# Joined softmax maps in attention C, output weights loaded early, and an MLP that writes its rows token by token

## The chip, the core and the metric

The kernel runs on one core of a Trainium2 chip. The metric is device time in microseconds (us) of one launch, the median of several executions. Engines are named as the profile names them: PE is TensorE, DVE VectorE, ACT ScalarE, POOL GpSimd, SP the sync engine that issues the DMAs.

## The reference, cut to what matters

Two layers over 1024 tokens of width 1024, all in float32. Each layer has four kinds of attention heads side by side (A, B, C, D), an output projection, and an MLP.

```python
for l in range(2):
    h = rms_norm(x, norm_mix_pre[l])
    ua, ub, uc, ud = jnp.split(h @ w_in[l], SPLITS, axis=-1)
    oa, ob, oc, od = attention A, B, C, D of ua, ub, uc, ud    # each normed
    mix = jnp.concatenate([oa, ob, oc, od], axis=-1) @ w_out[l]
    x = x + rms_norm(mix, norm_mix_post[l])
    h = rms_norm(x, norm_mlp_pre[l])
    f = jnp.square(jax.nn.relu(h @ w_up[l])) @ w_down[l]       # 1024 -> 4096 -> 1024
    x = x + rms_norm(f, norm_mlp_post[l])
```

Attention C is the one that the change rewrites. Each of its 4 heads has two softmax maps over the same values, with a bias that falls with distance:

```python
lam = exp(sum(lq1 * lk1)) - exp(sum(lq2 * lk2)) + lambda_init
sc  = einsum('bhmqd,bhmsd->bhmqs', q, k) * scale - slopes * dist   # m = 0, 1
p   = softmax(sc, axis=-1)
a   = p[:, :, 0] - lam * p[:, :, 1]
o   = einsum('bhqs,bhsd->bqhd', a, v)
```

## The kernel before

The program is a row of stages, each a block in which every engine has its own instruction list; the lists are tied together by counting semaphores, and every stage ends in a barrier of all engines (`end_stage`). There is no planner: the order on each engine is the order in which the Python code writes it. The layer loop runs twice. In it come the projection and attention of A, then two passes (head pairs) of the projection and attention of C, two of D, then B, then the output stage, the MLP stage and a norm stage.

float32 products are made of halves. A value is split into a high half (a rounded copy in the type fp32r) and a low half (value minus high half), and a product is three passes: high by high, high by low, low by high. ACT makes high halves, DVE or POOL the low ones. A matmul streams 512 columns past a 128 x 128 stationary tile.

**Attention C** (`attention_stage` with `combine`). A pass has 2 heads with 2 maps each, so 4 maps of 8 query tiles: 32 map tiles. For each, PE makes 128 x 1024 scores (two matmuls) in PSUM. DVE adds the bias and takes the maximum in one operation (L605). ACT takes the exponential and its row sum (L574). PE transposes the eight 128 x 128 parts (L293), in two pieces of four. ACT and DVE split each piece (L558, L616). PE multiplies by the values, for two query tiles at a time (L519), and folds (L532). At the end of a map, DVE scales by the row sums (L628) and, after the second map of a head, joins the two outputs with lambda (L630).

**The stage before attention C** (`pair_stage`). PE makes three units of 128 output columns from the layer's input and weights that come over a ring of two slots. SP issues the weights, then `extra_dma`: the distance table of 1920 columns (L976), the slopes (L977), and the lambda vectors (L979 to L981). ACT makes the two bias tables from it (`biases`, L987), and only then the first high half `c_p_h` (L925). SP waits for that half and then issues 32 copies that stack the halves for the score products (L897). The stage waits for the last of them.

**Output stage.** `mix` holds a token tile of 128 tokens and 1024 features at a time. Each tile is squared, summed by head group, scaled (`mix_sums`, `mix_norm`), transposed by PE (`turn_mix`) and split (`mix_high`, `mix_low`). w_out comes in eight blocks over a ring of three (L1445), is scaled by the gains and split by ACT and DVE (`weight_high` L1527, `weight_low` L1623). PE multiplies tiles 0 and 1 together block by block while the weights come, then tiles 2 to 7 one by one. Behind each product follow a norm, the addition to x (`post_norm`, L1630 and L1635), a second norm (`pre_norm`, L1643), a transposition and a split for the MLP. DVE begins its list with a wait for eleven small loads of gains.

**MLP stage.** In each of 4 chunks of 1024 hidden columns there are 8 up units and 8 down units, each of 48 matmuls, all with a weight tile stationary and activations streamed, so that results have features on the partitions. After an up unit follow relu (ACT, L1758), square (DVE, L1772) and the split (L1761, L1775). After a down unit DVE adds to `mlp_out_t` (L1782). Weights of 128 columns come over a ring of two slots, split by ACT (L232) and POOL (L241).

**Norm stage** (`norm_stage`, tag `mlp_post`). It loads x and the gains, PE transposes `mlp_out_t` back to tokens, and for each of 8 token tiles follow the norm (L400), the addition to x (L405), the next layer's norm (L413), a transposition, and the split (L386, L419).

## Time and profile before

| | us |
|---|---|
| median of 3 runs | 3611.39 (3608.26 to 3613.09) |
| the profiled execution | 3608.68 |
| its span, first to last instruction | 3607.0 |

| engine | busy us | share |
|---|---|---|
| PE | 3198.7 | 89% |
| DVE | 1512.7 | 42% |
| ACT | 1347.0 | 37% |
| POOL | 437.0 | 12% |

The mean granted clock of PE is 0.932 of full speed. It has two levels, 1.2 and 2.4 GHz. Shares are means over stages with different limits. The windows below say how busy each engine is in one stage; the order of instructions in time says what it waits for.

### The profile page before, as it was taken

Reading aid. Unit: us, or ns where it says so; the run is one execution under the profiler, and the core shown is the slowest. Engines: PE = TensorE matmul, PEld = TensorE weight load, DVE = VectorE, ACT = ScalarE, POOL = GpSimd, SP = SyncE. Lnnn points to the kernel's source line nnn. Section 1 sums busy time; section 2 is a strip of 40 time slices with the busy share of each in tenths; the row PEclk is TensorE's granted clock in tenths of the full one; section 3 lists DMA queues with packets and bytes.
Section 4 is the critical chain, followed back from the end, with each engine's and each line's share of the span. In section 5 each row is a group of like instructions: output and inputs, shape, how many; then the busy total and the mean of one; then the engine's idle time right before and its main releaser. Section 6 shows DMA issues by size and latency. Waiting matters only on the chain. (4 is left out here: it accounts for less than half of the span.)

```text
span 3607.0 us, 41597 instructions
## 1 busy us (share of the span) xinstructions
PE 3198.7 (89%) x16304; PEld 2668.6 (74%) x16304; DVE 1512.7 (42%) x1975; ACT 1347.0 (37%) x2210; POOL 437.0 (12%) x209
## 2 busy tenths in 40 slices
PE   7789888878789999999769889888878899999996
PEld 5678776767568888888658777776766688888885
DVE  4848554366542111112358476443765311111115
ACT  3648553455322121212227466443653221211113
POOL 1000000110002222222110000001100122222220
PEclk9899999889899999999879999898889999999998
DMA  5030333100321111111230312331012211111112
GB/s 151 1 76 1 77 64 64 28 15 7 105 70 47 47 47 46 52 47 47 105 65 1 76 30 48 64 64 34 10 32 91 65 53 47 47 47 47 46 52 105
DMA packets 250646, 191.32 MB, mean 53 GB/s; under 512 B 65480, under 2 KB 229320, under 8 KB 250442
## 3 DMA queue, kind: packets, MB, share of 16 engines
q1 hardware_dynamic: 250494, 189.38, 19.5%
q8 instruction: 95, 1.56, 0.2%
q14 instruction: 45, 0.37, 0.0%
q10 hardware_dynamic: 12, 0.02, 0.0%
HBM read 141.12 MB, written 24.89 MB: 46 GB/s over the span
## 5 line engine op out<-in xcount | busy, mean ns | idle before, releaser
L241 POOL TENSOR_TENSOR w_l_m<-w_raw_m,w_h_m 128x1024 fp32r<-128x1024 f32 (+2 forms) x136 | 313.6, 2306 | 1655.5 <-ACT w_h_m L232 1655.5
L249 PE MATMUL u_ps<-h_hi,w_h_m 128*128 128x512 f32 x1024 | 406.9, 397 | 17.3 <-POOL w_l_m L241 17.3
L250 PE MATMUL u_ps<-h_lo,w_h_m 128*128 128x512 f32 x1024 | 407.3, 398 | 0.0
L250 PE MATMUL u_ps<-up_l,w_h_m 128*128 128x512 f32 x1024 | 398.4, 389 | 0.0
L249 PE MATMUL u_ps<-up_h,w_h_m 128*128 128x512 f32 x1024 | 398.4, 389 | 0.0
L232 ACT ACTIVATE w_h_m<-w_raw_m 128x1024 fp32r<-128x1024 f32 (+2 forms) x136 | 135.9, 1004 | 578.7 <-PE u_ps L253 562.5
L1782 DVE TENSOR_TENSOR mlp_out_t<-mlp_out_t,u_ps 128x1024 f32<-128x1024 f32 x64 | 78.1, 1221 | 591.8 <-PE u_ps L253 591.8
L253 PE MATMUL u_ps<-h_hi,w_l_m 128*128 128x512 f32 x1024 | 323.1, 397 | 0.0
L253 PE MATMUL u_ps<-up_h,w_l_m 128*128 128x512 f32 x1024 | 315.3, 389 | 0.0
L1772 DVE TENSOR_TENSOR m_square<-m_relu 128x1024 f32<-128x1024 f32 x64 | 78.4, 1226 | 515.5 <-ACT m_relu L1758 515.5
L249 PEld LDWEIGHTS u_ps<-h_hi,w_h_m 128*128 128x128 f32 x1024 | 193.8, 189 | 64.3 <-POOL w_l_m L241 18.1
L1758 ACT ACTIVATE m_relu<-u_ps 128x1024 f32<-128x1024 f32 x64 | 65.6, 1025 | 467.8 <-PE u_ps L253 467.8
L250 PEld LDWEIGHTS u_ps<-h_lo,w_h_m 128*128 128x128 f32 x1024 | 193.5, 189 | 47.3
L253 PEld LDWEIGHTS u_ps<-h_hi,w_l_m 128*128 128x128 f32 x1024 | 193.5, 189 | 47.0
L249 PEld LDWEIGHTS u_ps<-up_h,w_h_m 128*128 128x128 f32 x1024 | 192.3, 188 | 40.1
L253 PEld LDWEIGHTS u_ps<-up_h,w_l_m 128*128 128x128 f32 x1024 | 192.2, 188 | 40.0
L250 PEld LDWEIGHTS u_ps<-up_l,w_h_m 128*128 128x128 f32 x1024 | 192.1, 188 | 40.0
L616 DVE TENSOR_TENSOR pt_l_c<-t_ps_c,pt_h_c 128x512 fp32r<-128x512 f32 x256 | 165.3, 685 | 17.4 <-ACT pt_h_c L558 16.6
L605 DVE CUSTOM_DVE_ANT_0 s_ps_c<-s_ps_c,alibi 128x1024 f32<-128x1024 f32 x128 | 157.0, 1229 | 15.1 <-PE s_ps_c L493 13.6
L574 ACT ACTIVATE prob_c<-s_ps_c,nmax_c 128x1024 f32<-128x1024 f32 x128 | 143.2, 1119 | 26.1 <-DVE nmax_c L605 26.1
L293 PE MATMUL t_ps_c<-ident,prob_c 128*128 128x128 f32 x1024 | 144.9, 285 | 8.8 <-DVE pt_l_c L616 8.1
L293 PEld LDWEIGHTS t_ps_c<-ident,prob_c 128*128 128x128 f32 x1024 | 120.8, 146 | 40.2 <-issue 23.3
(298 smaller groups left out, 6474.3 us busy)
## 6 DMA issues: line engine op xcount, KB each, us to landing
w_raw_m<-in_w_down SPq DMA_DIRECT2D x64, 512.0 KB, 4.0
w_raw_m<-in_w_up SPq DMA_DIRECT2D x56, 512.0 KB, 4.0
ow_raw<-in_w_out SPq DMA_DIRECT2D x16, 512.0 KB, 3.7
mix<-out_x SPq DMA_DIRECT2D x16, 512.0 KB, 4.4
out_x<-mix SPq DMA_DIRECT2D x16, 512.0 KB, 4.0
x_mlp_post<-out_x SPq DMA_DIRECT2D x16, 512.0 KB, 8.9
out_x<-x_mlp_post SPq DMA_DIRECT2D x16, 512.0 KB, 2.6
x_mix_pre<-in_x SPq DMA_DIRECT2D x8, 512.0 KB, 8.2
```

The costliest lines, as they stand in the source:

```text
L232: last = nc.scalar.activation(hi[0:rows, u % 2, cols, :], raw[0:rows, u % 2, cols, :], ACT.Copy)
L241: last = nc.gpsimd.tensor_tensor(lo[0:rows, u % 2, cols, :], raw[0:rows, u % 2, cols, :], hi[0:rows, u % 2, cols, :], ALU.subtract)
L249: nc.tensor.matmul(o, w_hi, x_hi[:, tok], start=first, stop=False)
L250: nc.tensor.matmul(o, w_hi, x_lo[:, tok], start=False, stop=False)
L253: ins = nc.tensor.matmul(o, w_lo, x_hi[:, tok], start=False, stop=last)
L293: last = nc.tensor.transpose(dst[:, i * P:(i + 1) * P], src_of(i), ident[:, :])
L574: nc.scalar.activation(prob[:, n % 2, 0:cnt * P], s_ps[:, n % 2, 0:cnt * P], ACT.Exp, scale=1.0 if tiles[n % NT][2] is None else -1.0, bia ...
L605: nc.vector.tensor_tensor_reduce(out=s, in0=s, in1=bias(m), scale=1.0, scalar=MIN_START, op0=ALU.add, op1=ALU.min, accum_out=nmax[:, n:n + ...
L616: nc.vector.tensor_tensor(pt_l[at], turned(p, k0, k1), pt_h[at], ALU.subtract) \
L1758: nc.scalar.activation(r_sb[:, :], u_ps[:, u % 2, :], ACT.Relu) \
L1772: nc.vector.tensor_tensor(s_sb[:, :], r_sb[:, :], r_sb[:, :], ALU.mult) \
L1782: nc.vector.tensor_tensor(ft[:, m, :], ft[:, m, :], u_ps[:, u % 2, :], ALU.add) \
```

## The change

1. Attention C gets a stage of its own, `difference_stage`. Both maps of a head are taken together for each query tile. Two scores, two maxima and two exponentials are made. DVE computes the ratio of lambda and the two row sums (`weigh`: a reciprocal and a `scalar_tensor_tensor` of one column). POOL multiplies the second map by it and adds the first, 1024 columns each. From there on one map is transposed, split, and multiplied by the values. There is one scaling for each head and no joining of outputs.
2. `extra_dma` of C loads the distance table twice, straight into the two bias tables, and `biases` scales them in place.
3. w_out is loaded whole during attention B (`fetch_w_out`, on SP).
4. In the output stage `mix_sums(0)` comes ahead of the wait for the small loads. Tile 0 is multiplied alone: first the two passes with high halves of the weights, then the pass with the low ones. All other tiles follow one by one. The first up unit's weights are loaded and split here.
5. The MLP has 8 chunks of 512 hidden columns. Up units are as before. The down products have activations stationary (128 tokens) and weights streamed (512 columns), so that results have tokens on the partitions; DVE collects them in `acc` by 512 columns. w_down comes in full rows. In the last chunk the norms, the addition to x, the transpositions and the splits follow each token tile. The norm stage behind the MLP is gone.

```diff
+        def difference_stage(maps, bias, mix_cols, mix, lam):
+            TURN_LAG, VALUE_LAG = 2, 4
+                    scores(0, 0)
+                    scores(0, 1)
+                    for n in range(n_all + VALUE_LAG + 1):
+                        if n + 1 < n_all:
+                            scores(n + 1, 0)
+                        if 0 <= n - TURN_LAG < n_all:
+                            turn(n - TURN_LAG, 0)
+                            turn(n - TURN_LAG, 1)
+                        if n + 1 < n_all:
+                            scores(n + 1, 1)
+                        s = n - VALUE_LAG
+                        if s >= 1 and s % 2 == 0:
+                            finish(s // 2 - 1)
+                        if 0 <= s < n_all:
+                            values(s // 2, s % 2)
...
+                @block.gpsimd
+                def _(pool):
+                    for n in range(n_all):
+                        pool.wait_ge(S["ratio_done"], n + 1)
+                        nc.gpsimd.tensor_scalar(second[:, n % 2, :], second[:, n % 2, :], ratio[:, 1, n:n + 1], 1.0,
+                                                ALU.mult, ALU.mult).then_inc(S["scaled"], 1)
+                        pool.wait_ge(S["scaled"], n + 1)
+                        nc.gpsimd.tensor_tensor(first[:, n % 3, :], first[:, n % 3, :], second[:, n % 2, :],
+                                                ALU.add).then_inc(S["combined"], 1)
...
+                    def weigh(n):
+
+                        dve.wait_ge(S["exp_done"], 2 * n + 2)
+                        after(nc.vector.reciprocal(ratio[:, 0, n:n + 1], z[:, 1, n:n + 1]))
+                        nc.vector.scalar_tensor_tensor(out=ratio[:, 1, n:n + 1], in0=z[:, 0, n:n + 1], scalar=lam,
+                                                       in1=ratio[:, 0, n:n + 1], op0=ALU.mult, op1=ALU.mult) \
+                            .then_inc(S["ratio_done"], 1)
...
+                    for n in range(n_all + VALUE_LAG + 1):
+                        if n + 1 < n_all:
+                            maximum(n + 1, 0)
+                        if n < n_all:
+                            weigh(n)
+                        if n + 1 < n_all:
+                            maximum(n + 1, 1)
+                        if 0 <= n - TURN_LAG < n_all:
+                            low(n - TURN_LAG, 0)
+                            low(n - TURN_LAG, 1)
...
-                            sp.dma_start(nd[:, :], a["distance"]).then_inc(S["const_landed"], 16)
+                            for j in range(2):
+                                sp.dma_start(alibi[:, j, :], a["distance"]).then_inc(S["const_landed"], 16)
...
+                        def fetch_w_out(sp):
+                            for k in range(KT):
+                                sp.dma_start(wo_raw[:, k, :], a["w_out"][layer][k * P:(k + 1) * P, :]) \
+                                    .then_inc(S["w_landed0"], 16)
...
                         turn_mix(0)
+                        pe.wait_ge(S["tt_lo"], 1)
+                        for k in range(KT):
+                            pe.wait_ge(S["w_hi"], k + 1)
+                            passes_of(0, k, ((h_hi, w_h), (h_lo, w_h)))
                         turn_mix(1)
-                        pe.wait_ge(S["tt_lo"], 2)
                         for k in range(KT):
-                            if k == KT // 2:
-                                turn_mix(2)
                             pe.wait_ge(S["w_lo"], k + 1)
-                            for t in range(2):
-                                last = products_of(t, k)
-                                if k == KT - 1:
-                                    last.then_inc(S["gemm_done"], 1)
-                        turn_mix(3)
-                        for t in range(2, NT):
+                            last = passes_of(0, k, ((h_hi, w_l),))
+                        last.then_inc(S["gemm_done"], 1)
+                        turn_mix(2)
+                        for t in range(1, NT):
...
+                    def down(ch, t, ks):
+                        d0 = 2 * t
+                        tok = slice(t * P, (t + 1) * P)
+                        done = 2 * NT * ch + d0
+                        if ks[0] == 0 and done >= 4:
+                            pe.wait_ge(S["acc_done"], done - 2)
+                        for k in ks:
+                            pe.wait_ge(S["up_lo"], ch * CK + k + 1)
+                            pe.wait_ge(S["d_lo"], ch * CK + k + 1)
+                            for lhs, rhs in ((up_h, d_h), (up_h, d_l), (up_l, d_h)):
+                                for n in range(2):
+                                    last = nc.tensor.matmul(d_ps[:, (d0 + n) % 4, :], lhs[:, k, tok],
+                                                            rhs[:, k, n * HALF:(n + 1) * HALF],
+                                                            start=(k == 0 and rhs is d_h and lhs is up_h),
+                                                            stop=(k == CK - 1 and lhs is up_l))
...
+                    for ch in range(CH):
+                        for u in range(CK):
+                            up(ch * CK + u)
+                        down(ch, 0, range(0, CK - 1))
+                        down(ch, 1, range(0, CK - 1))
+                        down(ch, 0, range(CK - 1, CK))
+                        down(ch, 1, range(CK - 1, CK))
+                        for t in range(2, NT):
+                            down(ch, t, range(CK))
+                            if ch == CH - 1 and t >= H_LAG:
+                                if t == H_LAG:
+                                    pe.wait_ge(S["relu_done"], NU)
+                                turn(t - H_LAG)
+                    for s in range(NT - H_LAG, NT):
+                        turn(s)
...
+                    for ch in range(CH):
+                        for k in range(ch * CK, ch * CK + CK):
+                            down_hi_weights(k)
+                        for n in range(ch * CK, ch * CK + CK):
+                            rectify(n)
...
-                norm_stage("mlp_post", ft, vec("norm_mlp_post"), vec("norm_mix_next"))
```

## Rows read from the trace of the kernel before

**Rows 1.** Windows: attention C, attention D, MLP. Busy us (instructions) by engine, clock, DMA.

```profile
core 0: us, PE busy (x) PEld busy (x) DVE busy (x) ACT busy (x) POOL busy (x), PEclk, DMA share, GB/s
268.00:363.00 95.00, 87.02 (x640) 77.59 (x640) 82.32 (x138) 75.22 (x144) 0.00 (x0) 0.95 0.00 1
...
556.00:584.00 28.00, 25.13 (x189) 22.25 (x190) 21.26 (x49) 20.88 (x55) 0.00 (x0) 1.00 0.00 1
...
1057.00:1767.00 710.00, 709.23 (x3072) 578.54 (x3072) 120.47 (x97) 131.01 (x131) 156.04 (x67) 1.00 0.16 46
```

**Rows 2.** PE in order of time (start us, us long): down units; output stage.

```profile
1178.95 0.39 PE L249 MATMUL u_ps<-up_h,w_h_m 128*128 128x512 f32 x1
...
1180.31 0.39 PE L249 MATMUL u_ps<-up_h,w_h_m 128*128 128x512 f32 x1
...
1006.90 0.63 PE L1471 MATMUL o_ps<-ow_h,h_hi 128*128 128x512 f32 x2
...
1008.30 0.63 PE L1471 MATMUL o_ps<-ow_h,h_hi 128*128 128x512 f32 x2
```

**Rows 3.** DVE in order of time, attention C.

```profile
306.89 1.23 DVE L605 CUSTOM_DVE_ANT_0 s_ps_c<-s_ps_c,alibi 128x1024 f32<-128x1024 f32 x1
...
309.23 1.23 DVE L605 CUSTOM_DVE_ANT_0 s_ps_c<-s_ps_c,alibi 128x1024 f32<-128x1024 f32 x1
```

**Rows 4.** ACT and PE in order of time, attention C.

```profile
308.95 1.11 ACT L574 ACTIVATE prob_c<-s_ps_c,nmax_c 128x1024 f32<-128x1024 f32 x1
...
310.99 1.14 ACT L574 ACTIVATE prob_c<-s_ps_c,nmax_c 128x1024 f32<-128x1024 f32 x1
...
308.93 1.09 PE L293 MATMUL t_ps_c<-ident,prob_c 128*128 128x128 f32 x8
...
310.80 0.55 PE L532 MATMUL o_ps_c<-fold,ot_c 128*128 128x64 f32 x4
```

**Rows 5.** POOL by line and form: xcount, busy us, mean ns of one.

```profile
L241 POOL TENSOR_TENSOR w_l_c<-w_raw_c,w_h_c 128x1024 fp32r<-128x1024 f32 x8 | 19.1, 2392 | 45.9 <-ACT w_h_c L232 45.7
...
L165 POOL TENSOR_SCALAR_AFFINE_SELECT ident<-ident 128x128 f32<-128x128 f32 x1 | 0.3, 292 | 0.2 <-POOL fold L163 0.2
...
L167 POOL TENSOR_SCALAR_AFFINE_SELECT fold<-fold 128x64 f32<-128x64 f32 x1 | 0.2, 238 | 0.0
```

**Rows 6.** DVE and POOL in order of time: before attention C, and in attention B's projection.

```profile
386.14 2.39 POOL L241 TENSOR_TENSOR w_l_c<-w_raw_c,w_h_c 128x1024 fp32r<-128x1024 f32 x1 [10.18 <-ACT w_h_c L232]
...
386.37 2.17 DVE L1002 TENSOR_TENSOR lam<-lam_sum 128x1 f32<-128x1 f32 x1
388.58 0.16 DVE L1005 TENSOR_TENSOR lam<-lam,lam_init 128x1 f32<-128x1 f32 x1
...
761.03 2.56 POOL L1281 TENSOR_TENSOR bh_rt<-bh_u,bh_cos_sin 32x1024 f32<-32x1024 f32 x1 [3.21 <-ACT bh_u L1312]
...
761.40 1.22 DVE L1353 TENSOR_TENSOR h_lo<-bh_u_ps,h_hi 64x1024 fp32r<-64x1024 f32 x1
```

**Rows 7.** DMA issues: KB each, median us from issue to landing.

```profile
distance<-in_distance SPq DMA_DIRECT2D x4, 960.0 KB, 5.7
```

**Rows 8.** ACT and SP in order of time, the stage before attention C.

```profile
380.43 3.69 ACT L987 ACTIVATE alibi<-distance,slope 128x1920 f32<-128x1920 f32 x2 [6.93 <-DMA slope<-in_slopes]
...
385.14 4.97 SPq L897 DMA_DIRECT2D c_q_s<-c_p_h  x8
```

**Rows 9.** PE and DVE in order of time: output stage and the MLP's first matmul.

```profile
906.54 1.97 PE L293 MATMUL m_ps<-ident,o_hm 128*128 128x128 f32 x8 [16.33 <-DVE o_hm L1610]
...
955.30 1.19 PE L1471 MATMUL o_ps<-ow_h,h_hi 128*128 128x512 f32 x2 [5.52 <-DVE o_y L1630]
...
1049.48 1.22 DVE L1649 TENSOR_TENSOR h_lo<-h_ps,h_hi 128x1024 fp32r<-128x1024 f32 x1 [3.12 <-ACT h_hi L1546]
...
1056.87 0.80 PE L249 MATMUL u_ps<-h_hi,w_h_m 128*128 128x512 f32 x1 [8.48 <-POOL w_l_m L241]
```

**Rows 10.** DVE in order of time, norm stage behind the first layer's MLP.

```profile
1800.81 1.28 DVE L400 SCALAR_TENSOR_TENSOR y_mlp_post<-y_ps_mlp_post,stat_mlp_post,g_post_mlp_post 128x1024 f32<-128x1024 f32 x1
...
1805.98 1.28 DVE L400 SCALAR_TENSOR_TENSOR y_mlp_post<-y_ps_mlp_post,stat_mlp_post,g_post_mlp_post 128x1024 f32<-128x1024 f32 x1
...
1819.00 1.23 DVE L419 TENSOR_TENSOR h_lo<-h_ps_mlp_post,h_hi 128x1024 fp32r<-128x1024 f32 x1 [1.98 <-ACT h_hi L386]
```

More of the change, by code:

```diff
@@ L423, in norm_stage, with attention_stage @@
             end_stage()
-        def attention_stage(tag, maps, tiles, mix_cols, mix, combine=None):
+        def attention_stage(tag, maps, tiles, mix_cols, mix, combine=None, fetch=None):
             n_all = len(maps) * NT
@@ L656, in build @@
         norm_stage("mix_pre", None, None, a["norm_mix_pre"][0:1, :], a["x"], background_copy)
-        with nc.Fori(0, DEPTH) as layer:
+        with nc.Fori(0, DEPTH) as layer, ExitStack() as layer_scope:
             def vec(name, lo=None, hi=None):
@@ L983, in biases @@
                         def biases(act):
-                            act.wait_ge(S["const_landed"], 32)
+                            act.wait_ge(S["const_landed"], 48)
                             for j in range(2):
-                                nc.scalar.activation(alibi[:, j, :], nd[:, :], ACT.Copy, scale=slope[:, j:j + 1])
+                                nc.scalar.activation(alibi[:, j, :], alibi[:, j, :], ACT.Copy, scale=slope[:, j:j + 1])
                             act.wait_ge(S["dve_step"], 2)
@@ L1449, in _ @@
                         sp.wait_ge(x_copied, 16)
-                        for t in range(4):
+                        for t in range(3):
                             residual(t)
-                        for t in range(2, NT + 1):
+                        for t in range(1, NT + 1):
                             if t + 2 < NT:
@@ L1465, in turn_mix @@
                             transposes(pe, m_ps, lambda k: hm[:, k * P:(k + 1) * P]).then_inc(S["tt_done"], 1)
-                        def products_of(t, k):
-                            tok = slice(t * P, (t + 1) * P)
-                            for lhs, rhs in ((h_hi, w_h), (h_hi, w_l), (h_lo, w_h)):
-                                for n in range(2):
-                                    last = nc.tensor.matmul(o_ps[:, t % 2, n * HALF:(n + 1) * HALF], lhs[:, k, tok],
-                                                            rhs[:, k, n * HALF:(n + 1) * HALF],
-                                                            start=(k == 0 and lhs is h_hi and rhs is w_h),
-                                                            stop=(k == KT - 1 and lhs is h_lo))
-                            return last
                         def turn(s):
@@ L1481, in turn, with passes_of @@
                             transposes(pe, h_ps, lambda k: hn[:, k * P:(k + 1) * P]).then_inc(S["tr_done"], 1)
+                        def passes_of(t, k, pairs):
+                            tok = slice(t * P, (t + 1) * P)
+                            for lhs, rhs in pairs:
+                                for n in range(2):
+                                    last = nc.tensor.matmul(o_ps[:, t % 2, n * HALF:(n + 1) * HALF], lhs[:, k, tok],
+                                                            rhs[:, k, n * HALF:(n + 1) * HALF],
+                                                            start=(k == 0 and lhs is h_hi and rhs is w_h),
+                                                            stop=(k == KT - 1 and pairs[-1] == (lhs, rhs)
+                                                                  and (rhs is w_l or len(pairs) == 3)))
+                            return last
@@ L1651, in low @@
                                 .then_inc(S["lo_done"], 1)
+                        mix_sums(0)
                         dve.wait_ge(S["const_landed"], 16 * 11)
@@ L1685, in _ @@
                                     low(NT - 2)
[L1686 removed]
+                                if t + 2 < NT:
                                     mix_norm(t + 2)
```

517 lines of the change are left out of this document (386 added, 131 removed).

## The prediction

> **What bounds the kernel now.** I read the granted clock and busy times in windows first, stage by stage, and then the order of instructions inside each stage. Times are of the profiled execution, 3608.7 us in all (span 3607.0), which is 2.7 us under the median of the three runs; the sum is made against it. The layer loop runs twice with the same pattern; the windows are of the first pass. The MLP window is the largest part and nothing but TensorE: 709.2 us busy of 710, 3072 matmuls, clock at full level [rows 1]. No edit that leaves these 3072 matmuls can gain inside it. Everything around it is bound elsewhere: attention C by VectorE (back to back, below), the norm stage behind the MLP by VectorE with TensorE mostly waiting, and the output stage by waits at its head.
>
> **Attention C, four executions (two pairs, two layers).** The window of one lasts 95 us, of which 94.5 are the stage [rows 1]. It works through 32 map tiles. VectorE goes from one maximum to the next in 2.34 us (maximum, two low halves) [rows 3]; with the scaling of outputs that is 2.45, and the stage runs at 2.5. The change handles two maps in one round: two maxima, two low halves, where there were four. VectorE per round: 2.34 + 1.15 for the second maximum (its 1.23 less the overlap of 0.08) + 0.35 for the two tiny operations of `weigh` (a free one takes 0.16 [rows 6], twice, with the wait between) + 0.15 until the second score is there, + 0.11 for `divide`: 4.1. ScalarE: exponential 1.1, two high halves 0.95, second exponential 1.1, lift 0.2: 3.4 [rows 4]. TensorE: four scores 0.93, eight transposes and eight value products 1.87 [rows 4], finish 0.2: 3.0. GpSimd gets a multiplication by a scalar and an addition of 1024 columns. The addition has a row: 2.39 for two inputs [rows 5]. A one-input multiplication has none. The nearest rows are one-input selections: 54 ns more for 64 more columns, so 0.84 ns a column and 0.29 + 0.75 = 1.05 us for 1024 [rows 5]; the far end is the two-input price, 2.39. I take 1.05, because what is shared with the selection is the number of inputs. GpSimd's round is then 3.44 plus 0.25 of handovers = 3.7, below VectorE's.
>
> `weigh` ends in an operation with two SBUF inputs. Such an operation stretches while GpSimd works: 2.17 us for one column, ending when GpSimd's operation does; one that reads PSUM keeps its 1.22 inside a GpSimd operation [rows 6]. The maxima and low halves all read PSUM, so only `weigh` is held, with the second maximum and the low halves queued behind it. It comes 4.0 us after the last one and GpSimd ends 3.55 after it: no hold as long as GpSimd is below VectorE, and if it is above, the round is GpSimd's sum. The Trainium skill, page "SBUF — State Buffer", section "SBUF: two separate sides", speaks of an exclusive lock, held for a whole instruction, against operations of VectorE with two SBUF inputs; the trace agrees (2.17 against 1.22).
>
> The round is 4.15 (the old one also ran 2% over its sum). First `weigh` at 6.3 us (first score and maximum 2.5, two exponentials 2.5, next maximum 1.3), 15 rounds 62.3, 0.6 less at the end where no maximum follows, then 10.7 to drain (GpSimd 3.6, transposes and halves 2.5, values 2, lift to scaling 2.2, the rest 0.4): 78.7. Gain 15.8 each, **-63** in all. Bounds: round 4.0 gives -73; GpSimd at twice 2.39 gives a round of 5.1 and a stage of about 96, +5 in all.
>
> **The stage before it, four times.** `extra_dma` now sends the distance table twice, 960 KB more on SP's queue ahead of the slopes and lambda vectors. One such transfer took 5.7 us to land alone [rows 7]; behind others I take 5. ScalarE waits for the slopes (6.93 idle before `alibi` [rows 8]) and has the first `p_h` behind it; SP's 32 stack copies start when that is done, at 385.14, and at 0.63 us each fill the time to the end of the stage [rows 8]. Nothing hides the delay, since SP is last. **+20** (0 if the transfers share bandwidth better, 28 at most).
>
> **Output stage, twice.** w_out loads during attention B, whose SP queue is empty: nothing. In the output stage the first transposes started at 906.54 after waiting for the small gain loads [rows 9]. `mix_sums(0)` moves ahead of that wait, so they start 4 us earlier. The first product then starts near 907 with one tile and two of its three passes, paced by ScalarE's high halves (1.04 each); by VectorE's low halves, four of which stand behind `mix_low(1)`, tile 0 ends near 925. Tile 1 waits for `turn_mix(2)`, behind them, and runs 929.6 to 940.8. Tile 2 starts near 942, where it started at 955.30 after 5.5 us of waiting for tile 0's norm [rows 9]. The rest keeps its order and its stalls. I take 14 per layer, **-28** (-20 to -34). SP is no longer held by the ring of three. The MLP unit loaded, and its ScalarE copy and GpSimd subtraction, lie in slack of ScalarE and an idle GpSimd.
>
> **MLP start.** TensorE idled 8.48 us until 1056.87 for the first weights [rows 9]; with them there it starts after the barrier, some 1.4 us past the last low half (1049.48 + 1.22): 4.8 per layer, **-10**. The next up unit needs its load and both halves by 11 us later: load 6, halves 3.5, fits.
>
> **MLP body.** 3072 matmuls as before. But the down products took 1.36 us per six, the output stage's 1.40 [rows 2]; the former stream activations past weights, the latter weights past activations, as the new `down` does. I take 1.40: 1536 x 0.0066 = 10 per layer, **+20** (0 if the shorter beat stays; nothing shown excludes it). Chunk changes: the four down splits wait for all products of the previous chunk, then need two loads behind GpSimd (about 11 us), under an up unit of 11.2; `rectify` stands behind them with a further unit of slack. VectorE's 128 evacuations of 0.6 us hide. Zero to 1 us a chunk; I take 0.
>
> **Norm stage removed.** From the last matmul (1766.2, the end of 709.2 from 1057) to the end of the last low half, 1820.2 [rows 1, 10], are 54 us. Now tiles come out token by token. Per tile VectorE does the old beat of 5.17 [rows 10] and two evacuations of 0.6: 6.4; TensorE 24 x 0.233 = 5.6, with a turn 6.5. So norms keep up with products. Past the pure products remain 1.4 (the gains land after the first product), five turns 4.5, and a tail of 17: evacuation, two norms of tile 7 with their squares, the low halves queued, and the last transposes at half clock. 22.7 in place of 54: 31.3 per layer, **-63** (-58 to -66).
>
> Sum: -63 + 20 - 28 - 10 + 20 - 63 = -124 (-123.5 unrounded). 3608.7 - 123.5 = 3485; on the scale of the median **3488 us**.
>
> **The rivals.**
> - GpSimd bound: the multiplication costs like a two-input operation, round 5.1, attention C gains nothing. 3488 + 68 = 3556. For it: no row of such an operation, two ALU steps in it. Against: the selection's slope. 0.17. The Trainium skill, "GPSIMD Engine Reference", section "Engine selection", advises VectorE for elementwise work and calls one-input operations roughly line-rate on GpSimd. By the first half of that rule the change is on the wrong engine, by the second this rival is wrong.
> - Short beat stays in `down`: 3468. 0.13.
> - TensorE's clock falls in attention C, since only 3.0 of 4.15 us are filled. At the lower level (1.2 in place of 2.4 GHz) eight transposes take 1.97 for 1.09 [rows 4, 9], a round about 5.5, the stage 101: +89, 3577. Against: attention D ran 28 us at full level with TensorE 25.1 busy and gaps in it [rows 1]. 0.05.
> - Slower: GpSimd's round is so long that attention C eats all gains. The rest gives -61, so each C stage may grow by 15 to 109.5, a round of about 6.0, from which it decides: a multiplication of 3.4 us. At 4.5 the round is 7.1, the stage 126, the total 3677. It needs a software path slower than any row. 0.05.
> - The rest, 0.05: output stage and tail gain half as much, 3525.
>
> **How the numbers follow.** Forecast 0.55 with its own range 3465 to 3515; rivals as given. The range takes in the short beat with the best of the other bounds (3450) and the first rival with a few us more (3565); outside lie the last two priced rivals and edges. What 0.2% is, 7 us, is about what a measurement tells from no change. Faster 0.93, same 0.02, slower 0.05.
>
> **What would show it.** GpSimd's multiplication near 1.05 us and `weigh` unstretched; attention C 79 us from first score to last scaling; first stack copy 5 us later after its stage's first load; output tile 2 starting 14 us sooner; 1.40 us per six down matmuls; 22 us from the last 44 us of products to the stage's end. Wrong if `weigh` is stretched each round, if down starts wait at chunk changes, or if the clock row shows half level in C.

## The result, and the profile after

The changed kernel takes **3463.28 us** (median of 4 runs, 3462.15 to 3464.52), the kernel before 3610.93 on the same chip: a ratio of 0.9592, 95% interval 0.9575 to 0.9608. The forecast was 3488, its range 3450 to 3565; of the narrower band that the prediction gave its main case, 3465 to 3515, the time misses the lower end by 2. The profiled execution has a span of 3462.8 us, 144.2 under that of before.

I divide those 144 us at the first matmul of each stage, as both traces show it (us, two layers together):

| stretch | forecast | measured |
|---|---|---|
| attention C, four times | -63 | -66.5 |
| the projection stage ahead of it, four times | +20 | +6.1 |
| output stage and start of the MLP | -28 and -10 | -38.6 |
| MLP body and norm stage | +20 and -63 | -45.4 |
| sum | -124 | -144.4 |

The windows of the changed kernel, its answer to [rows 1]: the two C stages of the first layer, the MLP, and the tail of norms behind its products.

```profile
core 0: us, PE busy (x) PEld busy (x) DVE busy (x) ACT busy (x) POOL busy (x), PEclk, DMA share, GB/s
270.00:350.00 80.00, 64.06 (x352) 48.13 (x352) 63.96 (x132) 56.81 (x104) 56.03 (x32) 0.84 0.00 1
395.00:473.00 78.00, 61.09 (x352) 45.69 (x352) 63.77 (x132) 56.59 (x104) 56.05 (x32) 0.90 0.00 0
1007.00:1700.00 693.00, 689.97 (x2971) 559.37 (x2972) 197.66 (x189) 134.80 (x140) 163.07 (x63) 1.00 0.17 53
1700.00:1757.00 57.00, 34.59 (x168) 28.00 (x167) 41.70 (x52) 25.26 (x45) 0.72 (x1) 0.78 0.40 125
```

The C windows hold 352 matmuls where there were 640. The MLP body is still nothing but TensorE. The surprise is the clock of the first line: 0.84 where before had 0.95.

**Attention C.** VectorE and GpSimd in order of time, one round at the full clock (start us, us long); answers [rows 3].

```profile
302.37 0.16 DVE L816 RECIPROCAL ratio_c<-z_c 128x1 f32<-128x1 f32 x1
302.57 0.22 DVE L817 SCALAR_TENSOR_TENSOR ratio_c<-z_c,lam,ratio_c 128x1 f32<-128x1 f32 x1
302.71 1.23 DVE L809 CUSTOM_DVE_ANT_0 s_ps_c<-s_ps_c,alibi 128x1024 f32<-128x1024 f32 x1
...
303.85 1.28 DVE L823 TENSOR_TENSOR pt_l_c<-t_ps_c,pt_h_c 128x512 fp32r<-128x512 f32 x2
305.05 1.22 DVE L809 CUSTOM_DVE_ANT_0 s_ps_c<-s_ps_c,alibi 128x1024 f32<-128x1024 f32 x1
...
306.19 0.16 DVE L816 RECIPROCAL ratio_c<-z_c 128x1 f32<-128x1 f32 x1
```

```profile
302.89 1.12 POOL L791 TENSOR_SCALAR second_c<-second_c,ratio_c 128x1024 f32<-128x1024 f32 x1 [0.23 <-DVE ratio_c L817]
304.10 2.39 POOL L794 TENSOR_TENSOR first_c<-first_c,second_c 128x1024 f32<-128x1024 f32 x1
306.71 1.12 POOL L791 TENSOR_SCALAR second_c<-second_c,ratio_c 128x1024 f32<-128x1024 f32 x1 [0.23 <-DVE ratio_c L817]
```

VectorE has no gap: `weigh` comes again after 306.19 - 302.37 = 3.82 us. GpSimd has 3.6 us of work in it and then waits 0.23 for the next ratio. The multiplication is 1.12. The ratio operation takes 0.22, unstretched.

Not every round is 3.82. GpSimd's rows show where the others are, in the first rounds of the same stage:

```profile
285.92 2.37 POOL L794 TENSOR_TENSOR first_c<-first_c,second_c 128x1024 f32<-128x1024 f32 x1
289.62 1.12 POOL L791 TENSOR_SCALAR second_c<-second_c,ratio_c 128x1024 f32<-128x1024 f32 x1 [1.32 <-DVE ratio_c L817]
290.82 2.37 POOL L794 TENSOR_TENSOR first_c<-first_c,second_c 128x1024 f32<-128x1024 f32 x1
```

290.82 - 285.92 = 4.90, and GpSimd waits 1.32. TensorE's granted clock is at the lower level, 1.2 GHz, from 267.4 for 27.3 us here, and from 393.7 for 17.1 us in the next pair; at the starts of the two C stages before it was 10.2 and 6.8. From addition to addition the mean over the 15 rounds is 4.07 in the first pair and 3.95 in the second.

How long that stretch lasts is not fixed by the code. Eight profiles on record run the same `difference_stage` without extra matmuls; the low clock at its start lasts 14 to 27 us in them, and the four stages take 327.4 to 332.2 us together. The profile used here has the longest, 332.2.

**The stage ahead of C**, ScalarE; answers [rows 8].

```profile
367.73 3.68 ACT L1191 ACTIVATE alibi<-alibi,slope 128x1920 f32<-128x1920 f32 x2 [9.36 <-DMA slope<-in_slopes]
```

It waits 9.36 us for the slopes, where it waited 6.93. The first stack copy comes 18.1 us after the stage's first matmul, 1.4 later than before.

**Output stage and the MLP's first matmul**, TensorE; answers [rows 9].

```profile
872.22 1.97 PE L299 MATMUL m_ps<-ident,o_hm 128*128 128x128 f32 x8 [12.26 <-DVE o_hm L1821]
876.56 1.22 PE L1685 MATMUL o_ps<-ow_h,h_hi 128*128 128x512 f32 x2 [2.38 <-DVE h_lo L1828]
...
912.98 0.70 PE L1685 MATMUL o_ps<-ow_h,h_hi 128*128 128x512 f32 x2
...
1007.47 0.76 PE L255 MATMUL u_ps<-h_hi,up_w_h 128*128 128x512 f32 x1 [3.43 <-PEq L129]
```

The transpositions wait 12.26 instead of 16.33. Tile 2 starts (912.98) 40.8 us after them, where it was 48.8. TensorE waits 3.43 before the MLP in place of 8.48.

**MLP**: the page's groups of matmuls (count, busy, mean ns), and two down matmuls six apart in order of time; answer [rows 2].

```profile
L255 PE MATMUL u_ps<-h_hi,up_w_h 128*128 128x512 f32 x1024 | 408.2, 399 | 7.2 <-PEq L129 6.9
...
L2014 PE MATMUL d_ps<-wd_h,up_h 128*128 128x512 f32 x1024 | 318.4, 392 | 4.4 <-DVE m_acc L2110 2.7
L2014 PE MATMUL d_ps<-wd_l,up_h 128*128 128x512 f32 x1024 | 315.8, 390 | 0.0
```

```profile
1725.61 0.62 PE L2014 MATMUL d_ps<-wd_h,up_l 128*128 128x512 f32 x2
...
1726.97 0.61 PE L2014 MATMUL d_ps<-wd_h,up_l 128*128 128x512 f32 x2
```

1.36 us per six: the short beat stayed though the sides have changed. The changes from up to down units and back come with no wait. TensorE waits elsewhere, at the third token tile of each chunk, for VectorE to have copied or added the first tile's product out of PSUM; that can start only when the last part of the first tile is through, and then only the last part of the second, 1.36 us of matmuls, is left to do:

```profile
1064.72 2.55 DVE L2108 COPY m_acc<-d_ps 128x512 f32<-128x512 f32 x4 [3.96 <-PE d_ps L2014]
...
1065.33 0.62 PE L2014 MATMUL d_ps<-wd_h,up_l 128*128 128x512 f32 x2
1066.06 0.73 PE L2014 MATMUL d_ps<-wd_h,up_h 128*128 128x512 f32 x2
```

From 1065.33 to 1066.06 are 0.73 us, where two matmuls take 0.45. Behind the last product, VectorE and TensorE (answer [rows 10]):

```profile
1727.66 1.27 DVE L2110 TENSOR_TENSOR m_acc<-m_acc,d_ps 128x512 f32<-128x512 f32 x2
...
1747.08 1.22 DVE L2157 TENSOR_TENSOR h_lo<-u_ps,h_hi 128x1024 fp32r<-128x1024 f32 x1 [2.05 <-ACT h_hi L2081]
```

```profile
1734.26 1.94 PE L299 MATMUL u_ps<-ident,mp_hn 128*128 128x128 f32 x8 [5.31 <-DVE h_lo L2157]
1739.44 1.94 PE L299 MATMUL u_ps<-ident,mp_hn 128*128 128x128 f32 x8 [3.24 <-DVE h_lo L2157]
```

The tail is 20.7 us, from 1727.58 (1726.97 + 0.61) to 1748.30. Its last transpositions run at 1.94, the lower level.

### The profile page after: what moved, and what is told of

Read it like the earlier page. It is cut to its first block and busy times, and to the rows that moved or that the text cites. A ratio compares the mean times of both kernels' runs of the same rounds, so it can differ in the third digit from the quotient of the medians.

```text
span 3462.8 us, 38563 instructions
## 1 busy us (share of the span) xinstructions
PE 3078.8 (89%) x15024; PEld 2515.7 (73%) x15024; DVE 1584.9 (46%) x2141; ACT 1271.2 (37%) x2042; POOL 679.8 (20%) x329
## 5 line engine op out<-in xcount | busy, mean ns | idle before, releaser
L255 PE MATMUL u_ps<-h_hi,up_w_h 128*128 128x512 f32 x1024 | 408.2, 399 | 7.2 <-PEq L129 6.9
L256 PE MATMUL u_ps<-h_lo,up_w_h 128*128 128x512 f32 x1024 | 407.4, 398 | 0.0
L259 PE MATMUL u_ps<-h_hi,up_w_l 128*128 128x512 f32 x1024 | 323.8, 397 | 0.0
L2014 PE MATMUL d_ps<-wd_h,up_h 128*128 128x512 f32 x1024 | 318.4, 392 | 4.4 <-DVE m_acc L2110 2.7
L2014 PE MATMUL d_ps<-wd_l,up_h 128*128 128x512 f32 x1024 | 315.8, 390 | 0.0
L2014 PE MATMUL d_ps<-wd_h,up_l 128*128 128x512 f32 x1024 | 315.4, 389 | 0.0
L255 PEld LDWEIGHTS u_ps<-h_hi,up_w_h 128*128 128x128 f32 x1024 | 193.9, 189 | 55.8 <-issue 7.6
L256 PEld LDWEIGHTS u_ps<-h_lo,up_w_h 128*128 128x128 f32 x1024 | 194.1, 190 | 47.0
L259 PEld LDWEIGHTS u_ps<-h_hi,up_w_l 128*128 128x128 f32 x1024 | 193.4, 189 | 47.4
L2014 PEld LDWEIGHTS d_ps<-wd_l,up_h 128*128 128x128 f32 x1024 | 192.2, 188 | 40.7
L2014 PEld LDWEIGHTS d_ps<-wd_h,up_l 128*128 128x128 f32 x1024 | 192.2, 188 | 40.4
```

The source lines that it names most:

```text
L255: nc.tensor.matmul(o, w_hi, x_hi[:, tok], start=first, stop=False)
L256: nc.tensor.matmul(o, w_hi, x_lo[:, tok], start=False, stop=False)
L259: ins = nc.tensor.matmul(o, w_lo, x_hi[:, tok], start=False, stop=last)
L2014: last = nc.tensor.matmul(d_ps[:, (d0 + n) % 4, :], lhs[:, k, tok], rhs[:, k, n * HALF:(n + 1) * HALF], start=(k == 0 and rhs is d_h and l ...
```

## The experiments

A ratio is to the kernel before on the same chip, with its 95% interval. The changed kernel stands at 0.9592.

**C alone.** `difference_stage`, its maps, `extra_dma` and `biases` put into the kernel before; nothing else.

```diff
-                        attention_stage("c", maps, tiles, ..., combine=lam[:, 0:1])
+                        difference_stage(maps, lambda j, i: alibi[:, j, ...], ..., mix, lam[:, 0:1])
```

> The kernel before, with the joined stage of C alone and the distance table loaded twice; output stage, MLP and norm stage stay as they were. Theory T1 (the two traces, read side by side): attention C gains 66 us in its four executions and the projection stage ahead of it loses 6, so 60 less than before, 3551. Theory T2 (the prediction's terms, -63 and +20): 43 less, 3568. Rival R: the stages share something (the clock after C, the barrier), and the parts of the change don't add up; then the time is more than 10 us from both.

3543.36 us, 0.9819 (0.9803 to 0.9835): 66 less than before, not 43. The interval is 6 us to either side, so 60 just fits and 43 does not. In the trace the four C stages are 69.9 shorter, the four stages ahead 6.5 longer. The medians leave 80 for the rest of the change, whose two rows in the table above give 84: the parts add up as closely as the interval can tell.

**GpSimd's multiplication with a second wide operand.**

```diff
-nc.gpsimd.tensor_scalar(second[:, n % 2, :], second[:, n % 2, :], ratio[:, 1, n:n + 1], 1.0, ALU.mult, ALU.mult)
+nc.gpsimd.tensor_tensor(second[:, n % 2, :], second[:, n % 2, :], ratio[:, 1, n:n + 1].to_broadcast([P, SEQ]), ALU.mult)
```

> The changed kernel, but GpSimd's multiplication of the second map reads a second tile-wide operand (the ratio, broadcast along the row) in place of a scalar. Theory T1: such an operation costs what the addition costs, 2.39 us in place of 1.12; GpSimd's round becomes 5.0 to 5.1 us in place of 3.82, GpSimd back to back, and each C stage grows from 79 to about 96; 15 rounds x 1.2 x 4 stages, less what the rounds at half clock already had: +60 to +72, 3523 to 3535. VectorE's ratio operation, 0.22 us now, is stretched in most rounds to the end of GpSimd's operation. Rival R1: the broadcast operand is read as a scalar would be, the operation stays near 1.1 to 1.3 us, and the time stays within 10 us of 3463. Rival R2: the stretched ratio operation delays the second maximum and so the next exponentials, the round goes beyond GpSimd's own sum, above 5.5 us, and the time above 3555.

3485.90 us, 0.9663 (0.9647 to 0.9679), 22 more. None of the three prices was right, the mechanism of T1 was. GpSimd and VectorE in order of time:

```profile
303.98 1.89 POOL L791 TENSOR_TENSOR second_c<-second_c,ratio_c 128x1024 f32<-128x1024 f32 x1
305.95 2.38 POOL L794 TENSOR_TENSOR first_c<-first_c,second_c 128x1024 f32<-128x1024 f32 x1
308.43 1.89 POOL L791 TENSOR_TENSOR second_c<-second_c,ratio_c 128x1024 f32<-128x1024 f32 x1
```

```profile
307.50 0.85 DVE L817 SCALAR_TENSOR_TENSOR ratio_c<-z_c,lam,ratio_c 128x1 f32<-128x1 f32 x1
308.28 1.22 DVE L809 CUSTOM_DVE_ANT_0 s_ps_c<-s_ps_c,alibi 128x1024 f32<-128x1024 f32 x1
```

The operation with a broadcast operand costs 1.89, neither 1.12 nor 2.39. GpSimd is back to back, its round 4.45. The ratio operation, started at 307.50, ends when GpSimd's addition does (308.33): 0.85 in place of 0.22. The four C stages grow by 30.0 together, 7.5 each: 15 rounds x (4.47 - 4.01) = 6.9. That the total is only 22 higher is B's projections, 7.6 us shorter here with a low clock of 10.2 us instead of 20.5 (see the run with TensorE kept busy). So the bound passes to GpSimd as the prediction's first rival had it; at 1.12 us it does not. A full two-input operation there was not run.

The Trainium skill, page "SBUF — State Buffer", section "SBUF: two separate sides", has VectorE's operations with two SBUF inputs excluded by GpSimd for a whole instruction; the 0.85 that ends with GpSimd's operation agrees.

**One distance table.** ScalarE scales the second half of `alibi` out of the first, then the first in place.

```diff
-for j in range(2):
-    sp.dma_start(alibi[:, j, :], a["distance"]).then_inc(S["const_landed"], 16)
+sp.dma_start(alibi[:, 0, :], a["distance"]).then_inc(S["const_landed"], 16)
...
-for j in range(2):
-    nc.scalar.activation(alibi[:, j, :], alibi[:, j, :], ACT.Copy, scale=slope[:, j:j + 1])
+for j in (1, 0):
+    nc.scalar.activation(alibi[:, j, :], alibi[:, 0, :], ACT.Copy, scale=slope[:, j:j + 1])
```

> The changed kernel, but the distance table is loaded once and ScalarE scales it out of the first half of the tile into the second, then in place. Theory T1 (the prediction): the second load holds up slopes and stack copies by 5 us a stage, so 20 us come back, 3443. Theory T2 (the trace after, where the stage is only 1.2 to 1.8 us longer than before): 6 us come back, 3457. Rival R: the two loads share the queue's bandwidth so that the slopes come no earlier, nothing comes back, 3463, and the 1.5 us a stage have another cause.

3455.55 us, 0.9574 (0.9557 to 0.9590). 20 us did not come back. The total can't tell 8 us from nothing, but the trace can: from first matmul of the stage to first score 40.2, 40.2, 40.3 and 40.4 us, with two loads 42.1, 41.4, 42.0 and 40.9. That is 5.4 for the second load in all four, T2. In the first pair of each layer attention C was also 1.5 to 1.8 shorter, with the low clock for 17.1 us in place of 27.3. I don't credit that to the edit: the run below that only moves the first tile's sums has 17.1 there too.

**Attention C with TensorE kept busy.** Extra matmuls into PSUM that nothing reads: 8 at the end of the stage ahead, and in `difference_stage`:

```diff
 for n in range(n_all + VALUE_LAG + 1):
+    if n < 4:
+        fill(6 if n < 2 else 3)
     if n + 1 < n_all:
         scores(n + 1, 0)
...
+    if n < 2:
+        fill(6)
     if n + 1 < n_all:
         scores(n + 1, 1)
```

> The changed kernel, with matmuls whose result nobody reads: 8 at the end of C's projection stage and 6 beside each pair of scores of the first rounds of attention C, where TensorE otherwise stands idle 2 us at a time. Theory T1: TensorE's clock at half level for 27 us (first pair) and 17 us (second pair) is due to these gaps, and sets the rounds of 4.7 to 4.9 us there; with the gaps filled the half level ends after some 7 us or does not come, rounds run at 3.8 from the start, and each stage is 3 to 6 us shorter: 3440 to 3452. Rival R1: the clock rises earlier, but the rounds there are set by something else (the ratio operation behind GpSimd), and the time stays within 4 us of 3463. Rival R2: the clock stays at half level in spite of it, the extra matmuls lengthen the rounds, and the time rises by 5 to 20 us.

3453.35 us, 0.9572 (0.9556 to 0.9588). GpSimd's additions at the place where they came 4.90 apart:

```profile
285.02 2.38 POOL L804 TENSOR_TENSOR first_c<-first_c,second_c 128x1024 f32<-128x1024 f32 x1
...
288.83 2.39 POOL L804 TENSOR_TENSOR first_c<-first_c,second_c 128x1024 f32<-128x1024 f32 x1
```

and the windows of the two stages:

```profile
270.00:346.00 76.00, 64.25 (x382) 50.26 (x382) 64.36 (x132) 56.37 (x104) 56.11 (x32) 0.98 0.01 1
392.00:467.00 75.00, 62.86 (x382) 48.90 (x382) 64.33 (x132) 56.36 (x104) 56.10 (x32) 1.00 0.00 0
```

3.81 from round to round, clock 0.98 and 1.00, and the stages 3.6, 2.2, 3.6 and 2.2 us shorter than in the changed kernel's profile: 11.6 together. The long rounds were the clock's. The size is less sure: that profile is the longest of the eight named above, and against the shortest of them the four stages gain 6.8. The medians differ by 10, with intervals that overlap, and 3453 lies 1 us above T1's range. This profile, the fastest of its four executions, has some 8 us less outside attention C too, in B's projections, where the low level lasted 10.2 us instead of 20.5; such stretches differ from profile to profile of kernels that are alike there, so I don't credit them to the edit.

**Both edits together.**

> The changed kernel with both edits that had gained: one distance table, and the extra matmuls (nobody reads them) that keep TensorE's clock up at the start of attention C. Theory T1: they are independent, one acts in the projection stage and one in the attention stage: 3463 - 6 - 11 = 3446, with up to 8 us less where the half-level stretches of attention B's projections fall short as in the profile of the extra matmuls alone. Rival R: with the stack copies earlier, the pause of TensorE before attention C is shorter and the clock falls less anyway; then both together give no more than one, 3453.

3444.25 us, 0.9540 (0.9524 to 0.9556), apart from the changed kernel's interval and from R's 3453: T1. Against it, attention C is 12.4 shorter and the stage ahead 3.9, in sum 16 of the 19.

**The rectifier left out**, in the changed kernel and in the kernel before.

```diff
-nc.scalar.activation(r_sb[:, :], u_ps[:, n % 2, :], ACT.Relu)
+nc.scalar.activation(r_sb[:, :], u_ps[:, n % 2, :], ACT.Copy)
```

> The changed kernel with the MLP's rectifier left out (ScalarE copies the up product unchanged), so that the squared rows that the down products read hold no zeros; the output is not the reference's. The question is why down matmuls kept the beat of 227 ns while up matmuls take 234. Theory D (data: half of the activations are zeros): down goes to 233 to 234 ns, as the up products have, 1536 x 0.0066 = 10 us a layer, 3463 + 20 = 3483. Theory P (place or pattern of the operands: which side is stationary, the reused columns): the data change nothing, down stays at 227 ns and the time within 5 us of 3463.

> The kernel before with the MLP's rectifier left out in the same way (the output is not the reference's); there the activations stream past stationary weights. Theory D: the 227 ns of its down matmuls become 233 to 234, +20 us, 3631. Theory P: they stay at 227, and the time within 5 us of 3611. If this one changes and the other doesn't, the zeros act only on the side that streams.

3459.93 us and 3608.58 us; the down matmuls keep 227 ns from start to start in both. Zeros are not the cause.

**Rectifier and square left out.**

```diff
-nc.vector.tensor_tensor(s_sb[:, :], r_sb[:, :], r_sb[:, :], ALU.mult)
+nc.vector.tensor_tensor(s_sb[:, :], r_sb[:, :], r_sb[:, :], ALU.max)
```

> The changed kernel with rectifier and square left out of the MLP (the up products reach the down products unchanged, signed and bell-shaped; the output is not the reference's). Theory D2 (the beat depends on the values, and squares, rectified or not, are easy ones): the down matmuls go from 227 to 233 or 234 ns, 3483. Theory P2 (it depends on where the operands lie or on which instructions surround them, not on values): they stay at 227, 3463.

3461.69 us. The page's group of this run, to be held against that of the changed kernel above:

```profile
L2014 PE MATMUL d_ps<-wd_h,up_h 128*128 128x512 f32 x1024 | 318.3, 392 | 4.3 <-DVE m_acc L2110 2.7
```

The same to 0.1 us in 318, and 227 ns from start to start. The values of the activations do not set the beat; those of the weights were not varied.

**w_out loaded late.** The loads during attention B are taken out; eight loads stand behind the small gain loads of the output stage instead, ScalarE waiting for each block.

```diff
+for k in range(KT):
+    sp.dma_start(wo_raw[:, k, :], wo[k * P:(k + 1) * P, :]).then_inc(S[LATE[k]], 16)
...
+act.wait_ge(S[LATE[k]], 16)
 nc.scalar.activation(w_h[:, k, :], w_raw[:, k, :], ACT.Copy, ...)
```

> The changed kernel, but the eight 512-KB rows of w_out are sent at the start of the output stage, behind the small gain loads, in place of during attention B. Theory T1: they land one after another some 3.6 us apart, so the last comes about 30 us into the stage where ScalarE now has all eight high halves 20 us into it; tile 0 and all behind it are 6 to 12 us later in each layer: 3475 to 3487. Rival R: tile 0's end is set by VectorE's norms and low halves as much as by the weights, the loads hide behind it, and the time stays within 5 us of 3463; then the early loading is not what gained, the order by single tiles is.

3461.73 us, 0.9587 (0.9571 to 0.9603): nothing lost, T1 is out. ScalarE in order of time:

```profile
870.49 1.15 ACT L1744 ACTIVATE ow_h<-wo_raw,o_g_col 128x1024 fp32r<-128x1024 f32 x1 [6.62 <-DMA wo_raw<-in_w_out]
...
873.25 7.47 ACT L1744 ACTIVATE ow_h<-wo_raw,o_g_col 128x1024 fp32r<-128x1024 f32 x7
```

Seven high halves run without a gap, so each block has landed when its turn comes, all eight within 14 us of the first issue (866.15). My 3.6 us a block was the time of one load from issue to landing; with all eight in flight they overlap.

**The first tile's sums behind the gain wait.**

```diff
-mix_sums(0)
 dve.wait_ge(S["const_landed"], 16 * 11)
 ...
-mix_norm(0)
 dve.wait_ge(S["gain_done"], 1)
+mix_sums(0)
+mix_norm(0)
```

> The changed kernel, but in the output stage VectorE waits for the small gain loads first and forms the sums of the first tile behind them, as the kernel before did. Theory T1 (the prediction): the first transposes start 4 us later in each layer and all behind them follow: 3463 + 8 = 3471. Rival R: the first products are paced by ScalarE's weight halves, which need the gains in either order, so only 0 to 2 us a layer come back: 3463 to 3467.

3464.07 us, 0.9603 (0.9587 to 0.9619): R. The first transpositions are 2.2 us later after attention B, but the first matmul of the MLP follows them 133.6 us later instead of 135.3. The edit puts back VectorE's order alone: between attention B's end and the transpositions the kernel before took 1.9 us more than this one, and VectorE waited there 2.26 for ScalarE's root, here 0.37.

**The first up unit's weights loaded in the MLP stage.**

```diff
-sp.dma_start(first_raw[:, :, :], full_unit(a["w_up"][layer][:, 0:P])[0][0][1]) \
-    .then_inc(S["w_landed0"], 16)
...
-    if u:
-        up_weights(u)
+    up_weights(u)
...
+up_lo_weights(0)
 up_lo_weights(1)
...
+up_hi_weights(0)
 up_hi_weights(1)
```

> The changed kernel, but the first up unit's weights are loaded and split at the start of the MLP stage, as the kernel before did. Theory T1 (the prediction): what the early load removed is TensorE's wait at the MLP's start, 8.5 us before and 3.4 now, so 5 us a layer come back: 3473. Rival R: the down weights' loads, which now share the queue at that moment, make the wait longer than it was before, 8 to 10 us a layer more: 3479 to 3483. Rival S: the second up unit sets the start anyway, and nothing comes back.

3478.54 us, 0.9644 (0.9628 to 0.9660): 15 more, 7.6 a layer, just under R's lower end (8.2 and 8.1 a layer in the trace). TensorE's first matmul:

```profile
1010.96 0.79 PE L255 MATMUL u_ps<-h_hi,up_w_h 128*128 128x512 f32 x1 [11.54 <-POOL up_w_l L1963]
```

It waits 11.54, which is 3 more than the 8.48 of before. But the edit does not put back what the kernel before did, which loaded and split the first quarter of the unit by itself. The first halves there, then here:

```profile
1055.60 0.42 ACT L232 ACTIVATE w_h_m<-w_raw_m 128x256 fp32r<-128x256 f32 x1 [6.15 <-DMA w_raw_m<-in_w_up]
...
1056.09 0.72 POOL L241 TENSOR_TENSOR w_l_m<-w_raw_m,w_h_m 128x256 fp32r<-128x256 f32 x1 [292.51 <-ACT w_h_m L232]
```

```profile
1007.44 1.06 ACT L2037 ACTIVATE up_w_h<-up_w_raw 128x1024 fp32r<-128x1024 f32 x1 [6.95 <-DMA up_w_raw<-in_w_up]
...
1008.57 2.34 POOL L1963 TENSOR_TENSOR up_w_l<-up_w_raw,up_w_h 128x1024 fp32r<-128x1024 f32 x1 [279.94 <-ACT up_w_h L2037]
```

ScalarE's half takes 0.64 us more and GpSimd's 1.62 more; the load took 4.47 from issue to landing in place of 3.44, which a larger load and the down weights' load right behind it may share. These make up the 3 us. So R's time nearly came out, but its reason, the shared queue, accounts for 1 us at most. The early load is worth the 5 us a layer that the traces showed (8.48 to 3.43) against the old split loading, and 8 against loading a whole unit late.

**TensorE kept busy at the other pauses too.** The kernel with both edits, and at each pause lines like

```diff
+heat(u_ps[:, 0, 0:HALF], h_hi[:, 0, :], 14)
 for u in range(2):
     products(pe, u_ps[:, u, :], ring, units, u, h_hi, h_lo)
```

> The kernel with one distance table and warmed attention C (3444), with matmuls that nobody reads also where TensorE stands idle for 4 to 15 us elsewhere: the start of every projection stage, the pause in attention A's projection, both ends of attention B's second projection, the head of the output stage, the end of the output stage and the tail of the MLP. Theory T1: each pause costs a stretch of 7 to 20 us at half level, and where TensorE sets the pace in that stretch (starts of projections, of attention B, of the MLP) half of it is lost; with the pauses filled some 15 to 30 us a layer come back: 3385 to 3415. Rival R1: the extra matmuls themselves run at half level and delay what follows by 2 to 3 us at each of some ten places a layer, which eats the gain: 3430 to 3460. Rival R2: the level falls at these places whatever TensorE does, and the time rises above 3460.

3440.96 us, 0.9537 (0.9521 to 0.9553): the fastest, but not told apart from the 3444 of the kernel with both edits. T1 is out, and the time is R1's. Windows (columns as above) of the kernel with both edits, then of this one, each first from attention D's end to attention B's start and then the whole span:

```profile
634.00:730.00 96.00, 70.63 (x313) 55.37 (x314) 38.22 (x33) 33.99 (x41) 22.16 (x11) 0.86 0.19 40
...
0.00:3443.00 3443.00, 3081.00 (x15176) 2524.73 (x15176) 1586.84 (x2141) 1270.94 (x2042) 680.80 (x329) 0.94 0.20 56
```

```profile
631.00:731.00 100.00, 81.36 (x359) 63.48 (x359) 38.23 (x33) 33.94 (x41) 22.17 (x11) 0.89 0.19 39
0.00:3440.00 3440.00, 3185.62 (x15728) 2610.41 (x15728) 1586.01 (x2141) 1270.21 (x2042) 679.32 (x329) 0.96 0.21 56
```

The time at the low level falls from 385 us to 242, and the span by 3. R1's delay shows at one place: from attention D's first score to attention B's the extra matmuls cost 4.1 us in the first layer, and 0.3 in the second, where the low stretch without them happened to last 20.5 us instead of 10.2. All other places together gave back 7.7. I take it that most of a low stretch lies over the pause itself or over work that other engines pace; that was not shown place by place.

## Why the prediction was right, point by point

**Attention C (-63, measured -66.5).** From first score to last scaling the stage takes 78.7 us in the first pair, exactly as forecast, and 76.9 in the second. The exact one is luck, by errors that cancel. The round at full clock is 3.82, not 4.15: my sum of VectorE's parts was 4.1 with 0.15 for a late score and 0.11 for scaling, which do not occur in a plain round, and 2% on top; VectorE runs without a gap. With the one round that holds a scaling (4.77) and the short last one (2.99), the 15 rounds would take 57.4 us, 4.3 less than forecast. Against this went 1.5 us of a longer drain (12.2 for 10.7), and the clock, which I had weighed only as a rival over the whole stage (5.5 a round, 3577). It fell for the first rounds alone, to rounds of up to 4.9, and cost 2.9 us in the first pair of this profile and some 1.1 in the second. Filling the pauses took the long rounds away, so their cause is shown; it gave 7 to 12 us over four stages, by the profile that one compares with.

**GpSimd** was priced at 1.05 from the slope of one-input rows; 1.12 measured, and `weigh` unstretched. The rival that GpSimd is the bound was real in kind: 0.77 us more on the multiplication made it so, though at a round of 4.45 and not 5.1.

**C's projection stage (+20, measured +6): mis-sized.** The term took a second load of 960 KB at 5 us "behind others", as if loads came one after another. ScalarE's wait grew by 2.4 us and the stage by 1.5. The lower bound, loads that share bandwidth, was the right end. The run with one table gives 5.4 back in all.

**Output stage and MLP start (-38, measured -38.6).** Right in sum, and in its two parts: 5.05 us a layer at the MLP's start for 4.8, and some 14 in the output stage for 14. A reason was wrong. The 4 us by which transpositions start earlier are there (12.3 of waiting instead of 16.3), but `mix_sums(0)` makes only 2.2 of them, and undoing its order cost nothing at the end of the stage. Tile 2 starts 12 us sooner after attention B, not 14. Loading w_out early was costed at nothing, and it is worth nothing. That leaves the 14 us a layer to the order by single tiles and the ring of three that is gone; no run takes either of them back, so this is argued from what is left and not shown.

**MLP body (+20, measured about 0 from the beat): wrong term.** I inferred from the output stage that streaming weights past activations costs 1.40 per six. It stays at 1.36; the rival "short beat stays", 3468, is the one that came true, 5 us above the result. Chunk changes, taken as 0, cost nothing. What was put at nothing and is not is VectorE's emptying of PSUM: I wrote that it hides, and at each chunk's third tile it makes TensorE wait, seven times 0.28 us and once 1.65 in the first layer. With 0.42 for one late up weight this is 4.0 us. The beats themselves are 1.0 ns longer in the up units and 0.5 in the down ones, 2 us a layer.

**Norm stage (-63).** With the body it is -45.4 where the sum says -43. In the first layer the norm stage gave 28.7 us where 31.3 were forecast: turns of some 4.6 and a tail of 20.7 stand in place of the 54 us, not 22.7 (whose parts add up to 22.9). So of the 10 that the body's beat did not cost, some 6 went to the waits and beats above and 2.6 to the tail.

On the scale of the profiled executions the forecast was 21 us high: two costs of 20 were charged that came to 6 and 0, attention C gave 3.5 more, and some 17 us of smaller costs in the MLP were not charged. The forecast lies near because these errors partly cancel.

## What to carry to other kernels

A duration from issue to landing is not a price per load: with loads in flight together the second one of 960 KB cost 1.5 us and eight of 512 KB cost nothing. Before an engine's lower clock is fought, ask whether that engine sets the pace there: filled pauses gave 7 to 12 us at the start of attention C, and 3 at all other places together. An experiment that takes an edit back has to be compared with the old trace as well: the first up unit, put back to the start of the MLP, was loaded whole where it had come in parts, and 3 of the 8 us were that. And the bound of a balanced round can pass to another engine by one operand: keep GpSimd's operations to scalar operands where its round is as close to VectorE's as here (0.23 us).

## What the runs showed of the hardware that was not expected

- A GpSimd operation on 1024 columns costs 1.12 us with a scalar operand, 1.89 with a second operand that is broadcast from one column, 2.38 with two full ones.
- Matmuls of 512 columns come 227 ns apart in the down products and 234 in the up products, whichever side is stationary, and with zeros, squares or signed values alike. `h_hi` or `h_lo` is read by the slow ones of the MLP, the projections and the output stage, on one side or the other, but not by the low-half score products of attention A, which are as slow (233 in the mean). Whether the place of a tile in memory or the weights' values do it was not tried; the cause is open.
- TensorE's clock stayed at 1.2 GHz for 27.3 us with TensorE busy for 18.2 of them, when the stage began with pauses of 1.1 to 1.8 us between scores; in other profiles of the same stage it was 17.1, and with the pauses filled 3.4.
- VectorE's low half of the MLP activations (two SBUF inputs) takes 2.22 us when it starts inside a subtraction of GpSimd, and ends 1.1 us after it; before the change it took 1.22. TensorE did not wait for it in the up units.
